# Router logits from the normalised rows with pre-scaled weights, and the two best experts found by counting ranks

## The reference, cut to what matters

```
mod = (cond @ ada_w[layer] + ada_b[layer])[:, None, :]
sh_m, sc_m, g_m, sh_f, sc_f, g_f = jnp.split(mod, 6, axis=-1)
...
h = _rmsnorm(x, gn[2]) * (1.0 + sc_f) + sh_f

def _moe(h, w_router, b_router, w_gu, w_down):
    logits = (h @ w_router).astype(jnp.float32) + b_router.astype(jnp.float32)
    top_vals, top_idx = lax.top_k(logits, TOP_K)
    top_w = jax.nn.softmax(top_vals, axis=-1)
    gates = jnp.sum(jax.nn.one_hot(top_idx, N_EXPERTS, dtype=jnp.float32) * top_w[..., None], axis=-2)
    out = jnp.zeros_like(h)
    for e in range(N_EXPERTS):
        out = out + gates[..., e:e + 1].astype(h.dtype) * _swiglu(h, w_gu[e], w_down[e])
    return out
```

## Time and profile before

| | us |
|---|---|
| median of 3 runs | 990.37 (989.41 to 991.37) |
| the profiled execution, its own time | 987.62 |
| its span | 986.0 |
| PE busy | 876.4 (89% of the span) |
| DVE busy | 698.8 (71%) |
| ACT busy | 534.0 (54%) |
| POOL busy | 29.6 (3%) |
| chain that ended last: PE, DVE, ACT | 80%, 11%, 5% |

### The profile page before, as it was taken

One profiled execution on the slowest core, in us unless ns is written; L12 is line 12 of the kernel. 1 busy time (PEld: TensorE's weight loads), 2 busy tenths in 40 slices (PEclk: granted clock), 3 DMA queues, 4 the chain that ended last, 5 costly groups with the idle time before them and its releaser, 6 DMA issues.

```text
span 986.0 us, 12279 instructions
## 1 busy us (share of the span) xinstructions
PE 876.4 (89%) x4633; PEld 744.4 (75%) x4633; DVE 698.8 (71%) x580; ACT 534.0 (54%) x544; POOL 29.6 (3%) x48
## 2 busy tenths in 40 slices
PE   3999979899998999779796789999999999999980
PEld 3999866799997787565475368888888888888870
DVE  4877475876668588543436468989898989888863
ACT  2244753443443234334224268787878787878751
POOL 1000030000000000000000100000000000000001
PEclk9799999899999898886597589999999999999995
DMA  9989465287778796599011559999999999999933
GB/s 354 376 298 381 173 257 213 99 313 272 278 276 285 262 373 243 185 420 374 0 44 43 191 178 359 370 388 385 379 380 371 401 352 412 352 408 356 391 135 130
DMA packets 45958, 282.44 MB, mean 286 GB/s; under 512 B 5834, under 2 KB 5837, under 8 KB 19554
## 3 DMA queue, kind: packets, MB, share of 16 engines
q1 hardware_dynamic: 40426, 266.70, 70.5%
q0 software_dynamic: 3600, 13.11, 3.4%
q10 hardware_dynamic: 1896, 2.13, 0.7%
HBM read 256.24 MB, written 25.69 MB: 286 GB/s over the span
## 4 chain that ended last, share of the span: by engine, by line
PE 80%; DVE 11%; ACT 5%; issue 2%; DMA 1%; ACTq 1%; POOL 1%; POOLq 0%; DVEq 0%
PE ps L1495 8%; PE ps L1496 8%; PE ps L1500 8%; PE ps L1201 5%; PE ps L1204 5%; PE ps L1203 5%; PE ps L1167 5%; PE ps L1168 5%; PE ps L1169 5%; PE ps L1512 4%; PE ps L1513 4%; PE ps L1518 4%; DVE acc L782 2%; PE ps L1426 1%; PE ps L1427 1%
## 5 line engine op out<-in xcount | busy, mean ns | idle before, releaser
L1056 DVE TENSOR_TENSOR w_lo<-ring,w_hi 128x2048 fp32r<-128x2048 f32 (+1 forms) x96 | 210.6, 2202 | 45.4 <-ACT w_hi L671 44.9
L466 ACT ACTIVATE w_hi<-ring 128x2048 fp32r<-128x2048 f32 (+2 forms) x58 | 109.6, 1893 | 211.8 <-PE ps L1204 106.7
L766 DVE TENSOR_TENSOR w_lo<-ring,w_hi 128x2048 fp32r<-128x2048 f32 (+2 forms) x58 | 131.1, 2263 | 104.0 <-ACT w_hi L466 104.0
L671 ACT ACTIVATE w_hi<-ring 128x2048 fp32r<-128x2048 f32 (+1 forms) x96 | 175.8, 1841 | 25.0 <-PE ps L1500 18.3
L1201 PE MATMUL ps<-hT_lo,w_hi 128*128 128x256 f32 x480 | 137.3, 286 | 3.5 <-DVE w_lo L766 2.5
L1203 PE MATMUL ps<-hT_hi,w_hi 128*128 128x256 f32 x480 | 136.7, 285 | 0.0
L1204 PE MATMUL ps<-hT_hi,w_lo 128*128 128x256 f32 x480 | 136.6, 285 | 0.0
L1495 PE MATMUL ps<-w_hi,xe_hi 128*128 128x512 f32 (+1 forms) x256 | 99.9, 390 | 4.3 <-DVE xe_lo L1106 4.3
L782 DVE SCALAR_TENSOR_TENSOR acc<-ring,cond,acc 128x2048 f32<-128x2048 f32 x42 | 99.3, 2364 | 3.1 <-issue 0.3
L1496 PE MATMUL ps<-w_hi,xe_lo 128*128 128x512 f32 (+1 forms) x256 | 98.2, 384 | 0.0
L1056 DVE TENSOR_TENSOR m_lo<-ring,m_hi 128x2048 fp32r<-128x2048 f32 (+2 forms) x48 | 92.7, 1931 | 6.4 <-ACT m_hi L671 6.4
(11 more groups left out here) (262 smaller groups left out, 1475.6 us busy)
## 6 DMA issues: line engine op xcount, KB each, us to landing
ring<-in_moe_w_gu SPq DMA_DIRECT2D x64, 1024.0 KB, 6.3
ring<-in_ada_w SPq DMA_DIRECT2D x48, 1024.0 KB, 6.3
ring<-in_moe_w_down SPq DMA_DIRECT2D x40, 1024.0 KB, 7.0
ring<-in_moe_w_gu SPq DMA_DIRECT2D x32, 768.0 KB, 8.2
ring<-in_ffn_w_gu SPq DMA_DIRECT2D x22, 1024.0 KB, 5.1
ring<-in_sb_w_in SPq DMA_DIRECT2D x12, 1024.0 KB, 7.7
ring<-in_ffn_w_down SPq DMA_DIRECT2D x11, 1024.0 KB, 6.0
x_rows<-blank SPq DMA_DIRECT2D x1, 8704.0 KB, 27.4
```

What stands on the lines that cost most here:

```text
L466: act.activation(w_hi[m % 2][:, 0:cols_n], ring[n % R][:, 0:cols_n], ACT.Copy).then_inc(hi_done, 1)
L671: act.activation(m_hi[k % NB][:, 0:n_c], ring[(N0 + k) % R][:, 0:n_c], ACT.Copy).then_inc(hi_done, 1)
L766: dve.tensor_tensor(w_lo[m % 2][:, 0:cols_n], ring[n % R][:, 0:cols_n], w_hi[m % 2][:, 0:cols_n].bitcast(F32), ALU.subtract).then_inc(free ...
L1056: dve.tensor_tensor(m_lo[k % NB][:, 0:n_c], ring[(N0 + k) % R][:, 0:n_c], m_hi[k % NB][:, 0:n_c].bitcast(F32), ALU.subtract).then_inc(free ...
```

## The change

- `mod_columns(3)` and the DVE step `mod_cols(3)` behind it move from the router to the beginning of MLA: PE does the 16 products directly behind those of v = 2, ahead of the transposes of `xhat` for MLA.
- The router no longer reads the modulated rows. `wr_mod` is `wr` times the scale, made on DVE in MLA. Shift times `wr`, plus the bias, is `lg_add`: 9 f32 products on PE in MLA behind the transposes of the latents, and one copy on DVE. `modulated(3)`, its cuts and the cut of `wr` are gone.
- For the logits PE transposes `xhat`, ACT and DVE copy it to `xT32` (two copies of 512 columns each), and 16 f32 products with `xT32` stationary and 8 columns moving give the logits with tokens on partitions. The transposes of the logits are gone.
- The two best experts come from ranks: each logit is compared with all 8, and the number above it is counted.
- `member`, `ones_r` and `before_r` are fp32r, so the five counting products are fp32r products.
- `elo(0, 0)` and `elo(0, 1)` move from ahead of the logits to behind the row numbers and weights.
- `br` is loaded as one row instead of one value to each of 8 partitions.
- POOL makes `earlier` (a mask of 64 values, one memset and one select) in place of `eight`.

```diff
@@ scalar
-            act.dma_start(br[:, :], b_router.rearrange("o e -> e o"), allow_slow_non_contiguous=True)\
-                .then_inc(s_small, 16)
+            act.dma_start(br[:, :], b_router).then_inc(s_small, 16)
...
-            modulated_hi(3)
-            act.activation(wr_hi[:, :, :], wr[:, :, :], ACT.Copy).then_inc(wr_cut, 1)
+            for c in range(TC):
+                act.wait_ge(xr_mm, 2 * c + 1)
+                act.activation(xT32[:, c, 0:4, :].rearrange("p k n -> p (k n)"), ps[:, 2 * c, :], ACT.Copy)\
+                    .then_inc(xr_a, 1)
@@ vector
+            dve.tensor_tensor(wr_mod[:, :, :], wr[:, :, :], scale[:, 3, :].unsqueeze(2).broadcast_to([P, DC, E]), ALU.mult)\
+                .then_inc(mod_r, 1)
             dve.wait_ge(cThi, 1)
             dve.tensor_tensor(cT_lo[:, :, :], cT[:, :, :], cT_hi[:, :, :].bitcast(F32), ALU.subtract).then_inc(cTlo, 1)
+            dve.wait_ge(bias_mm, 1)
+            dve.tensor_copy(lg_add[:, :], ps[:, 0, MLA_IN:MLA_IN + E]).then_inc(bias_ok, 1)
+            dve.tensor_copy(ones_r[:, :], ones[:, :])
+            dve.tensor_copy(before_r[:, :], before[:, :]).then_inc(mod_r, 1)
...
-            mod_cols(3, 4)
-            modulated(3)
-            dve.wait_ge(wr_cut, 1)
-            dve.tensor_tensor(wr_lo[:, :, :], wr[:, :, :], wr_hi[:, :, :].bitcast(F32), ALU.subtract).then_inc(wr_cut, 1)
+            for c in range(TC):
+                dve.wait_ge(xr_mm, 2 * c + 2)
+                dve.tensor_copy(xT32[:, c, 4:8, :].rearrange("p k n -> p (k n)"), ps[:, 2 * c + 1, :]).then_inc(xr_d, 1)
...
+            link(dve.tensor_tensor(lg[:, :, :], ps[:, 0, 0:TC * E].rearrange("p (c e) -> p c e", c=TC),
+                                   lg_add[:, :].unsqueeze(1).broadcast_to([P, TC, E]), ALU.add))
+            other = lg[:, :, :].unsqueeze(2).broadcast_to([P, TC, E, E])
+            own = lg[:, :, :].unsqueeze(3).broadcast_to([P, TC, E, E])
+            for c in range(TC):
+                dve.tensor_tensor(level[:, c, :, :], other[:, c, :, :], own[:, c, :, :], ALU.is_ge)
+            for c in range(TC):
+                ins = dve.tensor_tensor(above[:, c, :, :], other[:, c, :, :], own[:, c, :, :], ALU.is_gt)
+            link(ins)
+            link(dve.tensor_tensor(level[:, :, :, :], level[:, :, :, :],
+                                   earlier[:, :, :].unsqueeze(1).broadcast_to([P, TC, E, E]), ALU.mult))
+            link(dve.tensor_tensor(above[:, :, :, :], above[:, :, :, :], level[:, :, :, :], ALU.max))
+            link(dve.tensor_reduce(rank[:, :, :], above[:, :, :, :], AX.X, ALU.add))
+            dve.tensor_scalar(member[:, :, :], rank[:, :, :], 2.0, None, ALU.is_lt).then_inc(member_ok, 1)
@@ tensor
             mod_columns(2, 4)
+            mod_columns(3, 5)
             transpose_xhat(2)
...
+            for k in range(DC):
+                pe.matmul(ps[:, 0, MLA_IN:MLA_IN + E], shift[:, 3, k:k + 1].to_broadcast([P, P]), wr[:, k, :],
+                          start=(k == 0), stop=False)
+            pe.matmul(ps[:, 0, MLA_IN:MLA_IN + E], ones[0:1, :], br[0:1, :], start=False, stop=True).then_inc(bias_mm, 1)
```

More of the change, by code:

```diff
@@ L184, in trunk @@
         wr = sb("wr", [P, DC, E])
-        wr_hi = sb("wr_hi", [P, DC, E], F32R)
-        wr_lo = sb("wr_lo", [P, DC, E], F32R)
-        br = sb("br", [E, 1])
-        lg = sb("lg", [P, TC, E])
[L190 to L197, removed]
+        wr_mod = sb("wr_mod", [P, DC, E])
+        br = sb("br", [1, E])
+        lg_add = sb("lg_add", [P, E])
+        ones_r = sb("ones_r", [P, P], F32R)
+        before_r = sb("before_r", [P, P], F32R)
+        lg = sb("lg", [P, TC, E])
+        earlier = sb("earlier", [P, E, E])
+        rank = sb("rank", [P, TC, E])
+        one = sb("one", [P, 2, TC, E])
+        gap = sb("gap", [P, TC, E])
         diff = sb("diff", [P, TC])
         wt = sb("wt", [P, 2, TC])
-        member = sb("member", [P, TC, E])
+        member = sb("member", [P, TC, E], F32R)
         row_of = sb("row_of", [P, E])
@@ L965, in _ @@
             lo(M + 1)
+            mod_cols(3, 5)
             lo(M + 2)
@@ L1077, in _ @@
[L1077 to L1083, removed]
+            dve.wait_ge(bias_ok, 1)
@@ L1084, in _ @@
+            for r in range(2):
+                ins = dve.tensor_scalar(one[:, r, :, :], rank[:, :, :], float(r), None, ALU.is_equal)
+            link(ins)
+            link(dve.tensor_tensor(gap[:, :, :], one[:, 1, :, :], one[:, 0, :, :], ALU.subtract))
+            link(dve.tensor_tensor(gap[:, :, :], gap[:, :, :], lg[:, :, :], ALU.mult))
+            dve.tensor_reduce(diff[:, :], gap[:, :, :], AX.X, ALU.add).then_inc(wt_a, 1)
             dve.wait_ge(pos_mm, 1)
-            dve.wait_ge(member_ok, 1)
@@ L1442, in _ @@
                     product(M + 2 * g + h, 4 * h, [(0, 512, bank(g, 2))], hT_hi, hT_lo, h == 0, h == 1, g + h == 2)
-            mod_columns(3, 4)
-            transpose_xhat(3)
-            pe.wait_ge(hTlo, 16)
-            pe.wait_ge(wr_cut, 2)
-            for k in range(DC):
-                for a in (wr_lo, wr_hi):
-                    for b in (hT_lo, hT_hi):
-                        ins = pe.matmul(ps[0:E, 2, 0:T], a[:, k, :], b[:, k, :],
-                                        start=(k == 0 and a is wr_lo and b is hT_lo),
-                                        stop=(k == DC - 1 and a is wr_hi and b is hT_hi))
-            ins.then_inc(lgT_mm, 1)
-            pe.wait_ge(lgT_ok, 1)
-            for c in range(TC):
-                ins = pe.transpose(ps[:, 2, c * E:(c + 1) * E], lgT[:, c * P:(c + 1) * P], ident[0:E, 0:E])
+            for c in range(TC):
+                pe.wait_ge(xhat_done, TC * 3 + c + 1)
+                for b in range(2):
+                    for a in range(4):
+                        k = 4 * b + a
+                        ins = pe.transpose(ps[:, 2 * c + b, a * P:(a + 1) * P], xhat[:, c, k * P:(k + 1) * P], ident[:, :])
+                    ins.then_inc(xr_mm, 1)
+            pe.wait_ge(mod_r, 2)
+            for c in range(TC):
+                pe.wait_ge(xr_a, c + 1)
+                for k in range(DC):
+                    if k == 4:
+                        pe.wait_ge(xr_d, c + 1)
+                    ins = pe.matmul(ps[:, 0, c * E:(c + 1) * E], xT32[:, c, k, :], wr_mod[:, k, :],
+                                    start=(k == 0), stop=(k == DC - 1))
             ins.then_inc(lg_mm, 1)
@@ L1461, in _ @@
             for c in range(TC):
-                o = ps[:, 2, 32 + c * E:32 + (c + 1) * E]
+                o = ps[:, 0, 32 + c * E:32 + (c + 1) * E]
                 if c:
-                    pe.matmul(o, ones[:, :], member[:, 0, :], start=True, stop=False)
-                pe.matmul(o, before[:, :], member[:, c, :], start=(c == 0), stop=True)
+                    pe.matmul(o, ones_r[:, :], member[:, 0, :], start=True, stop=False)
+                pe.matmul(o, before_r[:, :], member[:, c, :], start=(c == 0), stop=True)
             for c in range(TC):
-                ins = pe.matmul(ps[:, 2, 48:48 + E], ones[:, :], member[:, c, :], start=(c == 0), stop=(c == TC - 1))
+                ins = pe.matmul(ps[:, 0, 48:48 + E], ones_r[:, :], member[:, c, :], start=(c == 0), stop=(c == TC - 1))
             ins.then_inc(pos_mm, 1)
```

51 lines of the change are left out of this document (23 added, 28 removed).

## The result

The changed kernel took 995.33 us in the median against 989.41 of the kernel before, run beside it: ratio 1.0058, with a 95% interval of [1.0035, 1.0081]. A second set of ten runs gave 991.80 against 990.84, 1.0023 [1.0002, 1.0044]; by these ratios the changed kernel is 5.7 and 2.3 us slower, by the medians 5.9 and 1.0. (In the first set one of the eleven runs took 2960.3 us, which the ratio leaves out, the others 991.96 to 1001.19.) The prediction was 988.9, between 985.0 and 992.0. The profiled execution took 992.37 us, its span 990.7; before it was 987.62 and 986.0.

The account below looks back on a forecast made before the run. PE-bound expert visits were a rigid block, so time moves with their start, set by the router chain. Sum: 4.6 - 8.5 - 1.25 - 1.05 + 4.7 = -1.5 us on the median 990.37, giving 988.9; range 985.0 to 992.0.

Parts of the forecast that it names:

- Start of MLA: PE ahead of MLA's transposes: 32 adaLN passes at the 1.2 GHz level delay them; +4.6 us, bounds +1.3 and +5.7.
- MLA, the rest: Bias products on PE and small DVE operations later in MLA hide in existing waits; 0 us.
- Logits: Router, last `xhat` to logits: transposes, copies and 32 passes, mostly at 2.4 GHz; -8.5 us, bounds -5.7 and -8.9.
- Rival 2: Clock stays low for the router's products on PE; price +3.2 us, total 992.1, chance 0.16.
- Ranks: DVE from logits to comparisons' end takes 2.0 us against 3.3; -1.25 us, bounds -0.3 and -1.6.
- counting: PE's five counting products take one pass each instead of two; -1.05 us, bounds 0 and -1.6.
- The two subtractions: Behind `row_in`, hidden on DVE, but two freed 1 MB loads delay the scatter; +4.7 us, bounds 0 and 5.25.
- Rival 4: Subtractions hold up POOL's scatter issues behind `row_in`; some +1 us, total 990, chance 0.06 shared with another rival.
- Start: Kernel's beginning: one-row `br` load might let DVE's first adaLN step begin sooner; taken 0, bounds -2.7 and 0.

Follow-up runs that it names:

- b_modcols: Kernel before with only `mod_columns(3)` and DVE's three small operations on it moved to the beginning of MLA; 992.23 us, ratio 1.0017.
- back_hold: Changed kernel with the two subtractions back ahead of the logits and SP waiting for `row_in` before the load of piece 6; 989.98 us, ratio 0.9985.
- sp_hold: Changed kernel with SP waiting for `xe_in` to land before the expert load of piece 6, subtractions unmoved; 986.71 us, ratio 0.9969.
- both_start: Changed kernel, subtractions back ahead of logits, `mod_columns(3)` and bias passes in later PE waits, `wr` and `br` loads behind the first norm's roots; 980.47 us.
- before_again: Kernel before, unchanged, profiled once more; span 986.1 us.
- after_third: Changed kernel, unchanged, run a third time; profiled span 990.4 us.

## Why the prediction was wrong

- **Start of MLA, +4.6: right in kind, too large.** The first execution had +4.8, but of the eight executions with the 32 passes seven have +2.4 to +2.7. The prediction let the clock fall about 3 us after dense work, as in the one trace it had. By stretches of 1 us it fell 2.1 us after it in the changed kernel's first execution (0.87 between 385 and 386) and 4.4 us in the second (0.66 between 391 and 392), and there more passes ran at 0.113 us. That the profiled execution came so near to +4.6 is luck.
- **MLA, the rest, 0: right within half a microsecond, as far as is known.** 135.05 to 136.01 in the seven executions with all of the change up to there, 133.26 to 135.41 in the four without the bias products and `wr_mod`: 1.4 us on the mean. But the seven all have the clock's late rise in the attention. Against the two others with the late rise (135.39, 135.41) the difference is 0.4 us on the mean, and with the early rise the moved columns alone make 0.2 (`b_modcols`). Whether it is chance that the rise was late in all seven is open, and the bias products were not tried by themselves.
- **Logits, -8.5: right (-8.8) in two executions, -6.0 in the others.** The mechanism is right, and so are the two prices, 0.113 and 0.216 us for a pass. Rival 2 (the clock does not come up) is no alternative kernel behaviour but happens in five of seven executions: 32 x 0.216 = 6.9 us, and 6.83 was measured. It was priced at 3.2 us, though 6.9 - 4.0 is 2.9; it costs 2.8 (6.13 to 8.93).
- **Ranks -1.25 and counting -1.05: right.** 6.85 to 4.46 is -2.4, against -2.3.
- **The two subtractions, +4.7 with an upper bound of 5.25: the step that failed.** It measured +9.0, +8.8 and +9.1. The part that the prediction sized, two loads against the scatter, is 4.6 us by itself in `back_hold`, and 4.7 was taken; so close a match is in part luck, since the loads started earlier there. Missing are three things: POOL's issues slowed by the subtractions (1.3), a third load that now runs beside `xe_in` instead of behind it (2.0), and 1.0 whose cause is open. The bound counted only the loads that the moved lines free. Yet the third load starts 16.0 us behind `row_in` in both kernels (568.90 - 552.87 and 563.10 - 547.05), and the prediction's own `xe_in`, issued 14 us behind `row_in` with 3.4 to land, would have met it. Rival 4 had the slowed issues in its sights, priced them well (some +1) and argued them away with the steady issues of the visits, which are plain transfers, not indirect ones. With +9.0 in the place of +4.7 the sum is +2.8, 993.2, past the upper end of the range. The Trainium skill (SBUF — State Buffer, section "Who interferes with whom") has the rule that a `tensor_tensor` with both inputs in SBUF contends with a GpSimd instruction that reads SBUF; with 1.76 and 1.89 instead of 0.95 us in `sp_hold`, where no load is near, the trace agrees.
- **Start, 0: right.** `br`'s issue took 5.88 us, and `both_start` shows that a start without it would give nothing: DVE's second step starts at 12.61 us there.

The terms as measured in the first execution: FFN's end -1.3, entry +4.8, MLA +1.8, logits -8.8, ranks and rows -2.4, scatter and load +9.0, rest +1.6, together +4.7, the difference of the spans. Between `before_again` and `after_third` it is +0.4, +2.5, +0.6, -6.1, -2.4, +9.0, +0.3, together +4.3. In either, the 9 us of the scatter are what the router's shorter chain is lost to. In the second, two more terms of the prediction are off, the entry by -2.1 and the logits by +2.5, and all but cancel.

## What to carry to other kernels

A subtraction that frees a ring buffer is also the trigger of a load: whoever moves it lists every load that then starts ahead of the next transfer on the path, also those that stay in place and meet this transfer once it is late. Where it has to stand there, a wait in the loading queue for the transfer that matters holds the load instead (`sp_hold`: 7.7 of 9 us back). Small f32 passes belong into PE's waits: 32 of them in a wait of 5.92 us took 6.99, and the clock was up for what followed. Ahead of work on the path they cost what no wait covers, 2.4 to 4.8 us here for the same 32.

## What the runs showed of the hardware that was not expected

- An indirect transfer's issue on POOL took 0.95 us alone and 1.76 and 1.89 us beside a `tensor_tensor` of 2048 columns with both inputs in SBUF, with loads near (the changed kernel) and without (`sp_hold`).
- Two loads of 1 MB beside the scatter (`back_hold`) turned the landing of each of its transfers from 3.7 us into 8.6 (median), more than the 4.6 by which the whole became later.
- The same code had the router's passes at 2.4 GHz in two of seven executions and at 1.2 GHz in five; this may be a part of why the changed kernel's median was 995.33 us in one set and 991.80 in the next.
- The place of the clock's rise in the attention is worth 2 us between executions of the kernel before (133.26 and 135.39 us in MLA).
